# Experts' blocks of 32 places on four column quarters of the array, in a fused attention and mixture-of-experts layer

## The chip, the core and the metric

The kernel runs on one core of a Trainium2 chip. The metric is the device time of one execution in microseconds, lower is better.

## What is computed

One decoder layer on 1024 tokens of width 1024, all float32: RMSNorm, two attention mixers in parallel and their gated merge, then RMSNorm and a routed mixture of 32 experts (SwiGLU, hidden width 512), and a last RMSNorm. The change is in the experts. Each token goes to one group of eight experts and to the best two of them:

```python
gsel = argmax(xt @ w_group + b_group)                  # one of 4 groups
ev, ei = lax.top_k(elog_g, 2)                          # two of its 8 experts
ew = softmax(ev) * gw                                  # their weights
y  = (silu(xb @ w1[e]) * (xb @ w3[e])) @ w2[e]         # for each (token, expert)
out = segment_sum(y * ew)                              # both rows of a token added
```

That makes 2048 pairs of token and expert; how many fall to an expert is known only at run time. W1 and W3 of an expert are 1024 x 512, W2 is 512 x 1024, 2 MB each.

## The kernel before, in words

All engines run hand-written programs that meet at semaphores. What comes before the experts (norms, projections, attention, merge, lines 400 to 900 of the five programs) isn't touched. The routing runs on VectorE tile by tile. GpSimd scatters each token's id into a table in memory, 1024 places for every expert (`scatter_ids`, line 1483), and VectorE adds up how many blocks each expert needs (lines 1322 to 1331, `starts_i`).

A block is up to 64 places (`SLOTS`, line 46) of one expert; every expert has at least one. For each block:

- GpSimd (loop at line 1516) copies the block's ids (1520), gathers its rows of the normed tokens into `xin` (1523), and loads the ids of the next block (`load_ids`, 1510). The rows lie in `hn_d` as two halves of 2 KB, so a block is 128 half rows on 128 partitions. `xin` has one buffer; the gather waits until TensorE has turned the rows before (`x_tr`). Places without a token are left out of the gather.
- TensorE (`expert`, line 844) multiplies the turned rows `xT` with W1 and W3 (line 856): the 64 places are the stationary operand and take half of the array's columns, so that two halves of the weights' columns run side by side, in two PSUM banks. Then it turns the next block's rows (`turn_rows`, 831), turns the hidden rows of its own block (864), and multiplies them with W2 (870).
- ScalarE computes the tanh (`gate_and_rows`, 1026), moves the turned rows out of PSUM (1032), copies the block's output (`put_rows`, 1037) and stores it in `rows_d` with two DMAs (1040). Before the next copy of an output it waits for the landing of that store (`y_st`).
- VectorE forms the SwiGLU product (1364, 1370) and moves the turned hidden rows (1374).

SyncE streams the weights: three experts are held at a time, and `load_expert` (331) for expert e + 3 waits until the blocks of e have used each of W1, W3 and W2. At the end GpSimd gathers two output rows for every token (1532), which are weighted, added and normed.

A float32 matmul stands in the trace as two records.

Of the kernel before, what the change touches and what calls it, by code (L numbers as in the profile page):

```python
# [32 lines left out]
P = 128  # L33
# [12 lines left out]
SLOTS = 64  # L46
MAXB = NE + 2 * SEQ // SLOTS
# [42 lines left out]
def build(nc, t, out):  # L90
# [16 lines left out]
    hn_d = scratch("hn_d", (2 * SEQ, D // 2))  # L107
# [11 lines left out]
    def ba(a, b, pat=None, /, **kw):  # L119
# [73 lines left out]
        we0 we1 we2 we3 we4 we5 we6 we7 we8 x_blk x_tr xT_evac mm1 mm3 tanh_done hid_done hT_ps hT_done y_ps y_evac y_st  # L193
        g_in0 g_in1 fin_in0 fin_in1 fin_in2 fin_in3 fin_in4 fin_in5 fin_in6 fin_in7 g_in2 g_in3 g_in4 g_in5 g_in6 g_in7 comb_std comb_done out_st0 out_st1 act_step h2_st0 h2_st1 gate_in gw_in0 gw_in1 gst0 gst1 hu_done loop_left gelu_arg tanh_gates nsink_done comb_sum gfin_in assigned wdiag_done fin_ps eps_ready wr_ready sel_done first_ps first_ids marks_done second_ps second_ids route_arg route_exp route_ps masks_ready tables y_free""".split()
# [53 lines left out]
    ZPARTS = 8  # L248
    steps_at, tile_done_at = [], {}
# [152 lines left out]
    def _(sp):  # L402
# [54 lines left out]
        for n in range(NGT):  # L457
# [85 lines left out]
    def _(pe):  # L543
# [252 lines left out]
        def first_rows(m):  # L796

            pe.wait_ge(S["sel_done"], m + 1)
            for h in range(2):
                mm = pe.matmul(PS[DH * h:DH * h + DH, 0, 0:2], sel[:, m, :], tok[:, h, m, :],  # L800
                               start=(m == 0), stop=(m == TT - 1), skip_group_check=True)
            return mm
# [18 lines left out]
        pe.wait_ge(S["marks_done"], 1)  # L821
        for m in range(TT):
            for c in range(2):
                for h in range(2):
                    mm = pe.matmul(PS[DH * h:DH * h + DH, 2, 0:2], mark[:, m, c, :], tok[:, h, m, :],
                                   start=(m == 0 and c == 0), stop=(m == TT - 1 and c == 1), skip_group_check=True)
        mm.then_inc(S["second_ps"], 1)
# [16 lines left out]
        def expert(e, nth, par):  # L844
# [715 lines left out]
```

## Time and profile before

| | us |
|---|---|
| median of 3 runs | 1650.41 (1647.76 to 1650.95) |
| the profiled execution | 1650.04 |
| its span, first to last instruction | 1648.4 |
| TensorE busy (matmul) | 1564.9, 95% of the span |
| TensorE weight loads | 848.1, 51% |
| VectorE busy | 560.9, 34% |
| ScalarE busy | 346.8, 21% |
| GpSimd busy | 300.6, 18% |
| DMA in the span | 328.42 MB, mean 199 GB/s |
| mean granted clock of TensorE | 0.988 |

All times are measured from the first instruction. The expert loop fills the stretch from 1050 to 1603 us. The span is 1.6 us shorter than the execution's own time; what the text works out from the trace is set against 1650.04. A busy TensorE is not one at its peak: matmuls overlap, and the records' ends are modelled. "Landing" is the time from the start of a DMA's issue until its semaphore is complete.

### The profile page before, as it was taken

How to read it: one execution, taken by the hardware profiler on the slowest of the kernel's cores; microseconds unless marked ns; L12 is line 12 of the kernel's file. 1: busy time of each engine (PE TensorE's matmuls, PEld its weight loads, DVE VectorE, ACT ScalarE, POOL GpSimd, SP SyncE). 2: the span in 40 equal slices, each digit the busy share in tenths (PEclk: the TensorE clock that was granted, in tenths of full speed). 3: DMA queues.
4: the chain of work that ended last, by engine and by line, in shares of the span. 5: the costliest groups of instructions: out<-in, count | busy, mean ns of one | idle time of the engine just before them, and what ended most of it. 6: DMA issues, size and time to landing. Idle time of an engine off the chain costs nothing.

```text
span 1648.4 us, 21863 instructions
## 1 busy us (share of the span) xinstructions
PE 1564.9 (95%) x7698; PEld 848.1 (51%) x7699; DVE 560.9 (34%) x1542; ACT 346.8 (21%) x859; POOL 300.6 (18%) x431
## 2 busy tenths in 40 slices
PE   7999998999999999998999999799899999999986
PEld 4554544444444444444444555566466666666652
DVE  4210004766566656654222354511011111111115
ACT  3000002443343443433000111111111111111113
POOL 2000001322222222222001001221121212121114
PEclk9999999999999999998999999999999999999997
DMA  9214621553111110103443821699999989999928
GB/s 236 67 56 62 125 78 58 166 181 114 45 32 26 45 33 26 46 13 90 161 136 103 357 107 74 235 416 419 419 419 418 386 352 407 416 421 417 415 85 306
DMA packets 135914, 328.42 MB, mean 199 GB/s; under 512 B 40046, under 2 KB 80398, under 8 KB 126640
## 3 DMA queue, kind: packets, MB, share of 16 engines
q1 hardware_dynamic: 117472, 297.98, 49.5%
q0 software_dynamic: 9984, 17.62, 3.2%
q10 hardware_dynamic: 8400, 12.07, 2.1%
q8 instruction: 34, 0.56, 0.1%
q14 instruction: 24, 0.20, 0.0%
HBM read 276.09 MB, written 55.25 MB: 201 GB/s over the span
## 4 chain that ended last, share of the span: by engine, by line
PE 83%; DVE 7%; DMA 5%; issue 2%; ACT 2%; POOL 1%; SPq 1%; POOLq 0%; ACTq 0%; DVEq 0%
PE PS L856 17%; PE PS L707 12%; PE PS L591 11%; PE PS L870 9%; PE PS L745 7%; PE PS L780 7%; PE PS L693 4%; PE PS L654 4%; PE PS L673 4%; PE PS L586 3%; DMA WA<-w 2%; PE PS L833 2%; DMA BA<-hn_d,ids 1%; POOL WA L1532 1%; PE PS L573 1%
## 5 line engine op out<-in xcount | busy, mean ns | idle before, releaser
L707 PE MATMUL PS<-WA 128*128 128x512 f32 x512 | 255.0, 611 | 2.2 <-ACT WA L967 1.6
L856 PE MATMUL PS<-WA,BA 128*64 128x256 f32 x2048 | 227.6, 379 | 2.9 <-DMA WA<-w 1.5
L856 PEld LDWEIGHTS PS<-WA,BA 128*64 128x64 f32 x2048 | 173.9, 137 | 63.9 <-issue 17.3
L591 PE MATMUL PS<-WA,BA 128*128 128x512 f32 x416 | 180.1, 593 | 2.9 <-DVE WA L1090 2.9
L1450 POOL TENSOR_SCALAR BA<-BA,rin,gates 128x640 f32<-128x640 f32 (+7 forms) x128 | 99.6, 781 | 270.8 <-DVE rin L1209 270.8
L1364 DVE SCALAR_TENSOR_TENSOR BA<-BA,PS 128x256 f32<-128x256 f32 x46 | 19.4, 422 | 340.8 <-ACT BA L1029 340.8
L591 PEld LDWEIGHTS PS<-WA,BA 128*128 128x128 f32 x416 | 78.6, 190 | 99.6 <-issue 96.2
L673 PEld LDWEIGHTS PS<-ident,BA 128*128 128x128 f32 x648 | 79.4, 144 | 94.1 <-issue 86.6
L870 PE MATMUL PS<-WA,BA 128*64 128x512 f32 x512 | 116.9, 597 | 9.7 <-DVE BA L1374 8.7
L707 PEld LDWEIGHTS PS<-WA 128*128 128x128 f32 x512 | 84.6, 190 | 78.4 <-issue 67.6
L957 ACT ACTIVATE BA<-PS,ngm 128x640 f32<-128x640 f32 (+7 forms) x128 | 89.9, 702 | 130.5 <-DVE ngm L1187 126.1
L780 PE MATMUL PS<-BA 128*128 128x512 f32 x256 | 113.1, 595 | 2.3 <-DVE BA L1245 2.3
L673 PE MATMUL PS<-ident,BA 128*128 128x128 f32 x648 | 101.2, 281 | 10.8 <-ACT BA L935 5.5
L745 PE MATMUL PS<-WA 128*128 128x512 f32 x256 | 110.1, 593 | 0.7 <-ACT WA L980 0.7
L856 PE MATMUL PS<-BA 128*64 128x256 f32 x896 | 101.4, 384 | 2.9 <-DMA BA<-w 2.9
L1219 DVE COPY BA<-PS 128x512 f32<-128x512 f32 (+3 forms) x126 | 62.7, 507 | 104.8 <-PE PS L673 104.7
L856 PEld LDWEIGHTS PS<-BA 128*64 128x64 f32 x896 | 76.9, 139 | 30.8 <-issue 8.2
L1186 DVE TENSOR_REDUCE mx<-PS 128x1 f32<-128x640 f32 (+7 forms) x128 | 90.6, 708 | 4.4
L1444 POOL TENSOR_TENSOR BA<-BA,rin 128x512 f32<-128x512 f32 (+1 forms) x32 | 31.5, 986 | 327.8 <-DVE rin L1196 327.8
L654 PE MATMUL PS<-WA 64*128 64x512 f32 (+3 forms) x384 | 75.9, 500 | 7.7 <-DVE pc L1177 4.0
L745 PEld LDWEIGHTS PS<-WA 128*128 128x128 f32 x256 | 48.6, 190 | 62.2 <-issue 60.7
L1520 POOL COPY ids<-ids 128x1 int32<-128x1 int32 x45 | 8.0, 178 | 386.7 <-PE PS L833 272.9
(249 smaller groups left out, 1548.4 us busy)
## 6 DMA issues: line engine op xcount, KB each, us to landing
WA<-w SPq DMA_DIRECT2D x66, 2048.0 KB, 25.3
BA<-w SPq DMA_DIRECT2D x30, 2048.0 KB, 27.6
rows_d<-WA SPq DMA_DIRECT2D x8, 2048.0 KB, 9.5
rows_d<-BA ACTq DMA_DIRECT2D x92, 128.0 KB, 6.8
WA<-w_in SPq DMA_DIRECT2D x16, 512.0 KB, 5.6
gates_d<-WA SPq DMA_DIRECT2D x32, 256.0 KB, 2.4
WA<-gates_d SPq DMA_DIRECT2D x8, 1024.0 KB, 5.4
BA<-w_in SPq DMA_DIRECT2D x26, 256.0 KB, 6.1
```

Source lines behind the costliest of these rows:

```text
L591: mm = pe.matmul(PS[:, j % 4, :], ws[:, c % 6, k, :], hnT[:, k, 512 * h:512 * h + 512], start=(k == 0), stop=(k == KT - 1))
L654: mm = pe.matmul(PS[:, bank, 0:e - a], qb[rows, h, q], kz[rows, w, k0 + a:k0 + e], start=True, stop=True)
L673: mm = pe.transpose(PS[:, 4 + n % 2, P * m:P * m + P], src, ident[:, :])
L693: mm = pe.matmul(PS[DH * g:DH * g + DH, bank, :], v_sb[:, w, kb, DH * g:DH * g + DH], pT[:, SLOT0[br] + n, g, :, :], start=(br == "A" and ...
L707: mm = pe.matmul(PS[:, 6, :], gw[:, j, k, :], hnT[:, k, 512 * hf:512 * hf + 512], start=(k == 0), stop=(k == KT - 1))
L745: mm = pe.matmul(PS[:, b0 + j, :], wbr[:, dt % 2, 4 * j + r, :], o[:, r, sl], start=(r == 0), stop=(r == REP - 1))
L780: mm = pe.matmul(PS[:, 2 * (i % 2) + n, :], mT[:, i, k, :], wout[:, k, 512 * n:512 * n + 512], start=(k == 0), stop=(k == KT - 1))
L856: mm = pe.matmul(PS[DH * h:DH * h + DH, bank, 0:256], xT[:, k, :], w[par][:, k, 256 * h:256 * h + 256], start=(k == 0), stop=(k == KT - 1))
L870: mm = pe.matmul(PS[DH * n:DH * n + DH, 3, :], hT[:, j, SLOTS * h:SLOTS * h + SLOTS], W2[par][:, 2 * h + j, 512 * n:512 * n + 512], start= ...
L957: last = nc.scalar.activation(PB[:, n % 3, 0:nk], src, ACT.Exp, bias=ngm[:, v, 0:1], scale=SC, accum_out=den[:, v, 0:1])
L1186: step(dve.tensor_reduce(mx[:, v, 0:1], s[:, 0:nk], X, ALU.max))
L1450: last = g.tensor_scalar(pr, pr, rin[:, v, 0:1], gates[:, i, col:col + 1], ALU.mult, ALU.mult)
```

## The change

- `SLOTS` is 32, and each expert has at least two blocks (`MAXB` follows).
- The 32 places take a quarter of the array's columns. `hidden_sums` multiplies with both halves of W1 and both of W3 in the four quarters, in one PSUM bank; `put_out` does W2 in four quarters of 256 columns.
- W2 of a block comes after the next block's W1 and W3 and its row transpositions. So the outputs of an expert's last block are computed inside the next expert's program, and once more after the loop.
- `hn_d` holds whole rows of 4 KB. A block's gather is 32 rows on 32 partitions; `turn_rows` is eight transpositions of 32 x 128. The output of a block is copied from PSUM by four copies of 32 x 256 into 32 rows, stored by one DMA.
- ScalarE computes the tanh on 64 partitions; VectorE's products are on 64 partitions, one of each, and one copy moves the turned hidden rows.
- GpSimd waits for the landing of the ids and of the gather before it copies the ids; the next ids' load stands ahead of the gather.
- The routing's second marks (`mark`, `place1`, line 825's matmuls) are gone: one product of selection and token numbers gives the ids of the first 64 places, of which the first two blocks' ids are taken.

The core of the diff; of the programs' loops the added lines are shown, those that go stand in the listing above:

```diff
-SLOTS = 64
-MAXB = NE + 2 * SEQ // SLOTS
+SLOTS = 32
+MAXB = 2 * NE + 2 * SEQ // SLOTS - 2
...
+    xin = BA[0:SLOTS, 8192:9216]
+    xT = ba(9216, 9472, "p (k n) -> p k n", k=KT)
+    xT_ps = PS[:, 7, 0:KT * SLOTS].rearrange("p (k n) -> p k n", k=KT)
+    th = BA[0:FIRST, 9728:9984]
+    hu = BA[FIRST:2 * FIRST, 9984:10240]
+    hv = BA[0:FIRST, 10240:10496]
+    hT = ba(10496, 10624, "p (j n) -> p j n", j=2)
+    hT_ps = PS[:, 2, 0:2 * FIRST].rearrange("p (j n) -> p j n", j=2)
+    ysb = BA[0:SLOTS, 10752:11776]
     fin_h = ba(12288, 20480, "p (t n) -> p t n", t=TT)
     fin_y = wa(0, 16384, "p (t k n) -> p t k n", t=TT, k=2)
...
-                sp.wait_ge(S[("mm1", "mm3", "y_ps")[j]], used)
+                sp.wait_ge(S[("mm13", "mm13", "y_ps")[j]], used)
...
         def turn_rows():
-            for c in range(4):
-                mm = pe.transpose(PS[:, 7, P * c:P * c + P], xin[:, P * c:P * c + P], ident[:, :])
+            for k in range(KT):
+                mm = pe.transpose(xT_ps[:, k, :], xin[:, P * k:P * k + P], ident[0:SLOTS, 0:SLOTS])
...
+        def hidden_sums(b, par, landed):
+            pe.wait_ge(S["xT_evac"], pe.snap(b + 1))
+            for n in range(2):
+                pe.wait_ge(S[f"we{3 * par + n}"], landed)
+            for k in range(KT):
+                for q in range(4):
+                    w = (W1, W3)[q // 2][par]
+                    mm = pe.matmul(PS[SLOTS * q:SLOTS * q + SLOTS, 0, 0:256], xT[:, k, :],
+                                   w[:, k, 256 * (q % 2):256 * (q % 2) + 256], start=(k == 0), stop=(k == KT - 1))
+            mm.then_inc(S["mm13"], 1)
+            pe.wait_ge(S["x_blk"], pe.snap(b * 16 + 32))
+            pe.sem_inc(S["turn_due"], 1)
+            turn_rows()
+        def put_out(n_done, par, landed):
+            pe.wait_ge(S["hT_done"], n_done)
+            pe.wait_ge(S["y_evac"], n_done)
+            pe.wait_ge(S[f"we{3 * par + 2}"], landed)
+            for j in range(2):
+                for h in range(2):
+                    for n in range(4):
+                        mm = pe.matmul(PS[SLOTS * n:SLOTS * n + SLOTS, 3, 0:256], hT[:, j, SLOTS * h:SLOTS * h + SLOTS],
+                                       W2[par][:, 2 * h + j, 256 * n:256 * n + 256],
+                                       start=(j == 0 and h == 0), stop=(j == 1 and h == 1))
+            mm.then_inc(S["y_ps"], 1)
+        def turn_hidden(b):
+            pe.wait_ge(S["hid_done"], pe.snap(b + 1))
+            pe.sem_inc(S["turn_due"], 1)
+            for j in range(2):
+                mm = pe.transpose(hT_ps[:, j, :], hv[:, P * j:P * j + P], ident[0:FIRST, 0:FIRST])
+            mm.then_inc(S["hT_ps"], 1)
+        def expert(e, par, landed, landed_before):
+            lo = pe.value_load(starts_i[0:1, bass.ds(e, 1)], min_val=0, max_val=MAXB - 2)
+            hi = pe.value_load(starts_i[0:1, bass.ds(e + 1, 1)], min_val=2, max_val=MAXB)
+            hidden_sums(lo, par, landed)
+            if landed_before is not None:
+                put_out(lo, (par - 1) % NW, landed_before)
+            turn_hidden(lo)
+            with pe.Fori(lo + 1, hi) as b:
+                hidden_sums(b, par, landed)
+                put_out(b, par, landed)
+                turn_hidden(b)
...
         def gate_and_rows(b):
+            act.wait_ge(S["mm13"], b + 1)
+            nc.scalar.activation(th, PS[0:FIRST, 0, 0:256], ACT.Tanh, scale=0.5).then_inc(S["tanh_done"], 1)
             act.wait_ge(S["x_tr"], b + 3)
...
+            nc.scalar.copy(xT, xT_ps).then_inc(S["xT_evac"], 1)
+        def put_rows(n_done, first):
+            act.wait_ge(S["y_ps"], n_done)
+            for n in range(4):
+                y = nc.scalar.copy(ysb[:, 256 * n:256 * n + 256], PS[SLOTS * n:SLOTS * n + SLOTS, 3, 0:256])
+            y.then_inc(S["y_evac"], 1)
+            act.wait_ge(S["y_evac"], n_done + 1)
+            act.dma_start(rows_d[bass.ds(first, SLOTS), :], ysb).then_inc(S["y_st"], 16)
         gate_and_rows(0)
+        gate_and_rows(1)
+        put_rows(1, 0)
+        with act.Fori(1, act.snap(total - 1)) as b:
+            gate_and_rows(act.snap(b + 1))
+            act.wait_ge(S["y_st"], act.snap(b * 16 + 16))
+            put_rows(act.snap(b + 1), act.snap(b * SLOTS))
+        act.wait_ge(S["y_st"], act.snap(total * 16))
+        put_rows(total, act.snap(total * SLOTS - SLOTS))
+        act.wait_ge(S["y_st"], act.snap(total * 16 + 16))
         act.sem_inc(S["loop_left"], 1)
...
+        total = dve.value_load(starts_i[0:1, NE:NE + 1], min_val=2 * NE, max_val=MAXB)
         with dve.Fori(0, total) as b:
+            dve.wait_ge(S["mm13"], b + 1)
             dve.wait_ge(S["tanh_done"], b + 1)
+            dve.scalar_tensor_tensor(hu, th, 1.0, PS[0:FIRST, 0, 0:256], ALU.add, ALU.mult).then_inc(S["hu_done"], 1)
             dve.wait_ge(S["hu_done"], b + 1)
+            dve.scalar_tensor_tensor(hv, hu, 0.5, PS[FIRST:2 * FIRST, 0, 0:256], ALU.mult, ALU.mult) \
+                .then_inc(S["hid_done"], 1)
+            dve.wait_ge(S["hT_ps"], b + 1)
+            dve.tensor_copy(hT, hT_ps).then_inc(S["hT_done"], 1)
...
-                               allow_slow_non_contiguous=True).then_inc(S["ids_in"], 16)
+            pool.dma_start(ids[0:SLOTS, 0:1], ids_d[bass.ds(row, SLOTS), 0:1],
+                           allow_slow_non_contiguous=True).then_inc(S["ids_in"], 16)
         pool.wait_ge(S["row_tab"], 1)
         load_ids(pool.value_load(block_row_i[0:1, 2:3], min_val=0, max_val=NE * SEQ))
-        total = pool.value_load(starts_i[0:1, NE:NE + 1], min_val=NE, max_val=MAXB)
+        total = pool.value_load(starts_i[0:1, NE:NE + 1], min_val=2 * NE, max_val=MAXB)
+        pool.wait_ge(S["ids_in"], 16)
+        g.tensor_copy(ids[0:SLOTS, 1:2], ids[0:SLOTS, 0:1]).then_inc(S["ids_held"], 1)
         with pool.Fori(2, total + 1) as b:
-            pool.wait_ge(S["ids_in"], pool.snap(b * 32 - 32))
+            pool.wait_ge(S["ids_held"], pool.snap(b - 1))
+            load_ids(pool.value_load(block_row_i[0:1, bass.ds(b + 1, 1)], min_val=0, max_val=NE * SEQ))
             pool.wait_ge(S["x_tr"], pool.snap(b + 1))
             pool.sem_inc(S["rows_due"], 1)
-            g.tensor_copy(ids[:, 1:2], ids[:, 0:1]).then_inc(S["ids_held"], 1)
-            pool.wait_ge(S["ids_held"], pool.snap(b - 1))
+            g.indirect_dma_start(xin, None, hn_d[:, :], bass.IndirectOffsetOnAxis(ap=ids[0:SLOTS, 1:2], axis=0),
+                                 bounds_check=SEQ - 1, oob_is_err=False).then_inc(S["x_blk"], 16)
+            pool.wait_ge(S["ids_in"], pool.snap(b * 16))
+            pool.wait_ge(S["x_blk"], pool.snap(b * 16 + 16))
             pool.sem_inc(S["rows_due"], 1)
-            g.indirect_dma_start(xin[:, :], None, hn_d[:, :], bass.IndirectOffsetOnAxis(ap=ids[:, 1:2], axis=0),
-                                 bounds_check=2 * SEQ - 1, oob_is_err=False).then_inc(S["x_blk"], 16)
-            load_ids(pool.value_load(block_row_i[0:1, bass.ds(b + 1, 1)], min_val=0, max_val=NE * SEQ))
+            g.tensor_copy(ids[0:SLOTS, 1:2], ids[0:SLOTS, 0:1]).then_inc(S["ids_held"], 1)
         pool.wait_ge(S["slots_done"], 1)
```

GpSimd's loop over the blocks before (`BA<-hn_d` is the gather, `ids<-ids_d` the loads of ids, TENSOR_LOAD reads the table of rows; ISA rows are waits and register work):

```order
L1518 REGISTER_ALU
L1520 COPY ids<-ids 128x1
L1521 REGISTER_ALU
L1523 DMA BA<-hn_d,ids 128x512
L1525 ISA
L1525 TENSOR_LOAD BA
L1525 ISA x2
L1510 ISA
L1510 DMA ids<-ids_d 64x1
L1510 ISA
L1510 DMA ids<-ids_d 64x1
```

and GpSimd's loop with the change:

```order
L1523 ISA
L1523 TENSOR_LOAD BA
L1523 ISA x2
L1513 ISA
L1513 DMA ids<-ids_d 32x1
L1524 REGISTER_ALU
L1526 DMA BA<-hn_d,ids 32x1024
L1528 REGISTER_ALU
L1529 REGISTER_ALU
L1531 COPY ids<-ids 32x1
```

The copy of the ids went from ahead of the gather to behind it, and the table's read and the load of ids from behind the gather to ahead of it.

TensorE's program of one block before (`128x128 x4` at L833 turns rows, L864 the hidden rows, L870 is W2):

```order
L856 MATMUL PS<-WA,BA 64x256 x32
L860 ISA
L833 MATMUL PS<-ident,BA 128x128 x4
L863 ISA
L864 MATMUL PS<-ident,BA 128x128
L863 REGISTER_ALU
L864 MATMUL PS<-ident,BA 128x128
L870 MATMUL PS<-WA,BA 64x512 x8
```

and TensorE's with the change, in a block that is not an expert's first (L840 is W1 and W3, L821 turns rows, L855 is W2, L865 turns the hidden rows):

```order
L840 MATMUL PS<-WA,BA 32x256 x32
L843 ISA
L821 MATMUL PS<-ident,BA 128x32 x8
L855 MATMUL PS<-WA,BA 32x256 x16
L865 MATMUL PS<-ident,BA 128x64 x2
```

W2 now stands ahead of the hidden rows' transpositions, and is that of the block before; the matmuls per block are 32 and 16 instead of 32 and 8.

## Rows read from the trace of the kernel before

**Rows 1.** The page, part 2: 40 slices of the span (41.2 us each)

```profile
DMA  9214621553111110103443821699999989999928
GB/s 236 67 56 62 125 78 58 166 181 114 45 32 26 45 33 26 46 13 90 161 136 103 357 107 74 235 416 419 419 419 418 386 352 407 416 421 417 415 85 306
```

**Rows 2.** The chain of waits, 1189 to 1213 us: start, length, what (matmul records)

```profile
1189.70 6.91 PE PS L856 x64
1196.61 0.59 PE PS L833 x4
...
1197.87 3.65 PE PS L870 x16
1201.53 6.91 PE PS L856 x64
```

**Rows 3.** Timeline, first W1 and last W2 block: start, length, what, idle before and releaser

```profile
1050.42 1.95 PE L856 MATMUL PS<-WA,BA 128*64 128x256 f32 x16 [1.32 <-ACT BA L1017]
...
1599.50 3.65 PE L870 MATMUL PS<-WA,BA 128*64 128x512 f32 x16 [0.28 <-DVE BA L1374]
1603.25 0.58 ACT L1037 COPY BA<-PS 128x512 f32<-128x512 f32 x1 [3.79 <-PE PS L870]
```

**Rows 4.** Timeline of TensorE, ahead of the loop

```profile
1031.95 1.10 PE L755 MATMUL PS<-ident,BA 128*128 128x128 f32 x8 [1.15 <-DVE BA L1307]
...
1036.31 0.39 PE L800 MATMUL PS<-winmask,cmpmask 128*64 128x2 bf16 x14
...
1044.69 1.02 PE L825 MATMUL PS<-winmask,BA 128*64 128x2 bf16 x32 [2.42 <-DVE BA L1319]
```

**Rows 5.** Timeline, the turn of one block on ScalarE, VectorE, TensorE and GpSimd

```profile
1205.02 0.38 ACT L1029 ACTIVATE BA<-PS 128x256 f32<-128x256 f32 x1 [2.81 <-PE PS L856]
...
1205.43 0.42 DVE L1364 SCALAR_TENSOR_TENSOR BA<-BA,PS 128x256 f32<-128x256 f32 x1 [7.51 <-ACT BA L1029]
...
1208.88 0.53 PE L864 MATMUL PS<-ident,BA 128*128 128x128 f32 x2
...
1209.45 0.18 POOL L1520 COPY ids<-ids 128x1 int32<-128x1 int32 x1 [8.88 <-DMA ids<-ids_d]
1210.49 1.07 POOL L1523 DMA_INDIRECT BA<-hn_d,ids  x1 [0.86 <-POOL ids L1520]
1211.57 1.08 POOL L1510 DMA_DIRECT2D ids<-ids_d  x2
```

**Rows 6.** Line 1525 (the table entry read), 1100 to 1280 us: count, ns min/median/max

```profile
L1525 POOLq TENSOR_LOAD <-BA x14: 283/287/307, 1109.4 to 1269.5; - x14
```

**Rows 7.** Timeline, a gather right behind another, at the end

```profile
1609.04 0.98 POOL L1532 DMA_INDIRECT WA<-rows_d,slots_i  x1 [0.30 <-issue]
```

**Rows 8.** Line 1523, the row gather, 1100 to 1280 us

```profile
L1523 POOL DMA_INDIRECT BA<-hn_d,ids x14: 1071/1075/1084, 1109.5 to 1269.6; - x14
...
DMA to landing us min/median/max: 5.9/8.3/9.0
```

**Rows 9.** Line 1523 after the last weights, 1572 to 1600 us (2 gathers)

```profile
DMA to landing us min/median/max: 2.2/2.7/3.3
```

**Rows 10.** Line 1040, the store of a block, 1100 to 1280 us

```profile
DMA to landing us min/median/max: 5.6/7.3/10.1
```

**Rows 11.** DMA queues and issues, 1100 to 1280 us

```profile
DMA packets 13397, 75.41 MB, mean 419 GB/s; under 512 B 2472, under 2 KB 2472, under 8 KB 10581
...
q1 hardware_dynamic: 8839, 68.65, 91.6%
...
WA<-w SPq DMA_DIRECT2D x23, 2048.0 KB, 31.3
```

**Rows 12.** Stretches around a wait of TensorE: busy PE, PEld, DVE, ACT, POOL, clock, DMA

```profile
1162.80:1165.20 2.40, 0.28 (x5) 0.21 (x6) 0.42 (x1) 0.38 (x1) 0.00 (x0) 1.00 0.97 383
1165.20:1168.60 3.40, 3.40 (x20) 1.89 (x18) 0.00 (x0) 0.00 (x0) 0.00 (x0) 0.50 1.05 430
```

**Rows 13.** Timeline, the wait in that place

```profile
1164.92 3.42 PE L856 MATMUL PS<-BA 128*64 128x256 f32 x16 [2.12 <-DMA BA<-w]
```

More of the change, by code:

```diff
@@ L798, in first_rows @@
             pe.wait_ge(S["sel_done"], m + 1)
[L799 to L802, printed above, removed]
+            return pe.matmul(PS[0:FIRST, 0, 0:2], sel[:, m, :], tok[:, m, :],
+                             start=(m == 0), stop=(m == TT - 1), skip_group_check=True)
         def keep_busy(count):
@@ L820, in _ @@
         pe.wait_ge(S["h2_done"], TT)
[L821 to L827, printed above, removed]
         keep_busy(10)
         def turn_rows():
-            for c in range(4):
-                mm = pe.transpose(PS[:, 7, P * c:P * c + P], xin[:, P * c:P * c + P], ident[:, :])
+            for k in range(KT):
+                mm = pe.transpose(xT_ps[:, k, :], xin[:, P * k:P * k + P], ident[0:SLOTS, 0:SLOTS])
             mm.then_inc(S["x_tr"], 1)
@@ L875, in _ @@
-        with pe.Fori(0, NE // NW) as e3:
+        def hidden_sums(b, par, landed):
[11 more added lines that the diff above has]
+            turn_rows()
@@ L876, in _ @@
+        for e in range(NW):
+            expert(e, e, 16, None if e == 0 else 16)
+        with pe.Fori(1, NE // NW) as e3:
             for par in range(NW):
-                expert(e3 * NW + par, e3 + 1, par)
+                expert(e3 * NW + par, par, pe.snap(e3 * 16 + 16), pe.snap(e3 * 16 if par == 0 else e3 * 16 + 16))
         for e in range(NE - NE % NW, NE):
-            expert(e, e // NW + 1, e % NW)
+            expert(e, e % NW, 16 * (e // NW + 1), 16 * ((e - 1) // NW + 1))
+        total = pe.value_load(starts_i[0:1, NE:NE + 1], min_val=2 * NE, max_val=MAXB)
@@ L1016, in _ @@
         act.wait_ge(S["x_tr"], 2)
-        nc.scalar.copy(xT_out, xT_ps).then_inc(S["xT_evac"], 1)
+        nc.scalar.copy(xT, xT_ps).then_inc(S["xT_evac"], 1)
         act.wait_ge(S["route_arg"], 1)
@@ L1285, in place @@
                 dve.wait_ge(S["first_ps"], 1)
-                dve.tensor_scalar(ids[:, 2:3], PS[:, 0, 0:1], PS[:, 0, 1:2], None, ALU.add).then_inc(S["first_ids"], 1)
+                for n in range(2):
+                    rows = slice(SLOTS * n, SLOTS * n + SLOTS)
+                    dve.tensor_scalar(ids[0:SLOTS, 2 + n:3 + n], PS[rows, 0, 0:1], PS[rows, 0, 1:2], None, ALU.add) \
+                        .then_inc(S["first_ids"], 1)
             step(dve.tensor_reduce(slot_f[:, m, :], pick, X, ALU.add))
@@ L1332, in _ @@
         dve.sem_inc(S["routed"], 1)
-        dve.wait_ge(S["second_ps"], 1)
-        dve.tensor_scalar(ids[:, 3:4], PS[:, 2, 0:1], PS[:, 2, 1:2], None, ALU.add).then_inc(S["second_ids"], 1)
         step(dve.tensor_tensor(G4[3][:, :, :], lgs[:, :, 0:NG], top[:, 0, :].unsqueeze(2).to_broadcast([P, TT, NG]), ALU.subtract))
@@ L1495, in _ @@
         scatter_ids(TT - 2)
-        pool.wait_ge(S["first_ids"], 1)
+        pool.wait_ge(S["first_ids"], 2)
         pool.wait_ge(S["hn_st"], 16 * TT)
-        g.indirect_dma_start(xin[:, :], None, hn_d[:, :], bass.IndirectOffsetOnAxis(ap=ids[:, 2:3], axis=0)) \
+        g.indirect_dma_start(xin, None, hn_d[:, :], bass.IndirectOffsetOnAxis(ap=ids[0:SLOTS, 2:3], axis=0)) \
             .then_inc(S["x_blk"], 16)
         scatter_ids(TT - 1)
-        pool.wait_ge(S["second_ids"], 1)
         pool.wait_ge(S["x_tr"], 2)
-        g.indirect_dma_start(xin[:, :], None, hn_d[:, :], bass.IndirectOffsetOnAxis(ap=ids[:, 3:4], axis=0)) \
+        g.indirect_dma_start(xin, None, hn_d[:, :], bass.IndirectOffsetOnAxis(ap=ids[0:SLOTS, 3:4], axis=0)) \
             .then_inc(S["x_blk"], 16)
```

116 lines of the change are left out of this document (22 added, 94 removed).

## The prediction

> **What bounds the kernel now.** I read the page's slices first, for where the time is, then the chain of waits over the expert loop, then what hides behind the chain: GpSimd's turn of one block and the landings of its DMAs.
>
> The slices [rows 1] show two things at once in the last third: the DMA engines are at 9 tenths and move about 419 GB/s, and this lasts for all of the expert loop. The chain [rows 2] shows one block of 64 places as 6.91 us of W1 and W3 (64 matmul records, two abreast, so 0.216 us per pair of records), 0.59 us of row transpositions, some 0.66 us for the hidden rows, and 3.65 us of W2 (16 records): 11.83 us from 1189.70 to 1201.53. The loop has 46 such blocks, from 1050.42 to 1599.50 + 3.65 = 1603.15 [rows 3], which is 552.7 us. 46 x 11.81 = 543.3; the other 9.4 are waits for weights. So TensorE sets the time, with the weights' DMA close behind it.
>
> What must be seen for this change is work that is hidden now. GpSimd copies the ids, then issues the gather 0.86 us later, then the loads of the next ids [rows 5]. The gather lands 8.3 us (median of 14; 5.9 to 9.0) after its start while weights stream [rows 8], and 2.2 to 3.3 us after it when they don't [rows 9]. One gather of 64 places is allowed 11.8 us today, so this shows nowhere as a wait of TensorE.
>
> **Number of blocks.** 46 blocks at 64 places with at least one for each of 32 experts means 14 experts with more than 64 places. Routing the reference's inputs gives 38 to 61 places to the other 18 and 66 to 94 to those 14. With 32 places and at least two blocks that is 18 x 2 + 14 x 3 = **78 blocks**. (The same 2048 places are filled; 2496 are computed, before 2944.)
>
> **TensorE's time for a block.** W1 and W3 still make 64 records of 256 columns, now four abreast: 16 x 0.216 = 3.46 us. No row shows four abreast. The bounds are 6.91 (two abreast, as now [rows 2]) and 3.46; I take the latter, since a pass of 256 columns takes its 0.216 us with the columns of both halves in use, and 32 short matmuls in 1.02 us [rows 4] show that four records can be issued in 0.13 us. The Trainium skill (TensorEngine Tiling (Array Packing), Tiling Modes) gives 128x32 as four tiles that run independently; no run here shows that. W2 is 32 records of 256 columns: 8 x 0.216 = 1.73 us. The eight row transpositions of 32 places lie between 8 x 0.028 = 0.2 us (the short matmuls of line 800) and 1.10 us (eight of 128x128 at line 755) [rows 4]; they load 128 columns each like the latter, I take 0.9. The two of the hidden rows: 0.4, from 0.53 for two wider ones [rows 5]. Sum 3.46 + 1.73 + 0.9 + 0.4 = **6.5 us**, and 78 x 6.5 = 507 us.
>
> The hidden rows' own chain (tanh 0.38, two products of 0.42 [rows 5], three handovers of about 0.1) is 1.5 us. It starts with the end of W1 and W3 and lies behind the row transpositions and W2 of the block before, 0.9 + 1.7 = 2.6 us: the wait of 0.3 us before W2 in each block [rows 3] goes, and it costs nothing as long as that cover stands.
>
> **The gather's round trip.** This is where the change adds a wait. xin has one buffer. In the new loop of GpSimd the copy of the ids waits for the landing of the gather before it, the load of the next ids stands between that copy and the next gather, and with them a read of the table. From a landing to the next gather's start: 0.25 us to the copy (semaphore and two queue instructions), 0.18 the copy, 0.86 until the next instruction that needs it [rows 5], 0.6 the table read (0.29 [rows 6] and the register work behind it), 0.55 the load of ids (half of 1.08 [rows 5]), 0.4 for the gather's own start (0.30 between two gathers [rows 7], and one more wait). That is 2.9 us; from below 1.9, if the table read and the start lie beside other work. Before, only 0.18 + 0.86 stood there.
>
> Then the landing. The gather has 32 rows of 4 KB instead of 128 of 2 KB. Bounds under weights: 8.3 us (nothing gained [rows 8]) and 5.6 us (the fastest store of 64 rows of 2 KB, the same 128 KB [rows 10]; its median is 7.3). I take 6.5, in the lower half, because the number of rows is a quarter. So a block takes 2.9 + 6.5 = **9.4 us** where weights stream, with bounds 1.9 + 5.6 = 7.5 and 2.9 + 8.3 = 11.2, and TensorE waits at line 821 (the row transpositions), holding W2 of the block before, the hidden rows and the next block. Where no weights stream the round trip is 2.9 + 2.3 = 5.2 us (2.3, near the shorter of the two landings [rows 9], for the fewer rows), less than 6.5: no wait.
>
> The weights of an expert are 6.29 MB. Their queue moved 68.65 MB in 180 us [rows 11], 381 GB/s, so they stream for 16.5 us per expert. TensorE needs 78 / 32 = 2.44 blocks, 15.9 us, without any wait; with waits it is slower than the weights, so these catch up, three experts are held, and each of the last 29 loads starts when an expert's buffers come free and ends before the next do. In 16.5 us there are 16.5 / 9.4 = 1.75 blocks, each 2.9 us over 6.5: 5.1 us. The rows of the first of them have landed up to 6.5 - 5.2 = 1.3 us early: 3.8 us remain. 29 x 3.8 = 110 us.
>
> **The clock.** After a wait of 2.12 us [rows 13] in a stretch at full clock, TensorE ran at 0.50 of it (1.2 GHz of 2.4) for 3.4 us [rows 12], which is 1.7 us of work lost. Waits of that length come once or twice per expert in this forecast. I count one, and half of it hidden in the next wait: 29 x 0.85 = 25 us. Bounds: 0, and 50 waits of 1.7 us, 85.
>
> **The rest.** The store: landing, four copies of 32 x 256 (0.38 each, from the 0.38 of line 1029 [rows 5], 1.5 together), 0.2 to the DMA, landing between 5.6 and 7.3: about 8.1 us, under 9.4 and hidden. It is what comes next if the gather turns out shorter than I say. The removed marks and 32 short matmuls (1.02 us, after 2.42 of waiting [rows 4]) let the loop start about 2 us earlier; the last block's four copies end 0.6 later than one of 0.58 [rows 3]. Bytes of the gathers are the same, stores shrink from 12.1 to 10.2 MB: not on the path. The value reads of each expert on TensorE's queue are issued while W2 runs: nothing.
>
> **The sum.** Loop 507 + 110 + 25 = 642 us against 552.7: +89. With -2 and +0.6 it is +88. The profiled execution took 1650.0 (span 1648.4), the median of the runs is 1650.4, so the two are alike: **1738 us**. A measurement of this kernel can't tell less than about 0.2% (3.3 us) from no change.
>
> **The rivals.**
>
> *A: the gather is short enough and the quarters pay (faster).* If the landing falls under 6.5 - 2.9 = 3.6 us with weights streaming, TensorE is never kept waiting: loop 507 + 9.4 = 516, time 1650 - 37 - 1 = 1612. From that landing on it decides. For it: landings of 2.2 to 3.3 us when the queues are empty [rows 9]. Against it: none of the 14 under load is below 5.9 [rows 8], and stores half their size aren't below 5.6 [rows 10]. The Trainium skill (DMA: Bandwidth & Descriptors, Anatomy of one DMA — SWDGE (gpsimd) path) fits a GpSimd DMA as 2.0 us and its bytes at 436 GB/s, which is an estimate of 2.3 us for 128 KB and would give this rival; rows 9 agree with it, rows 8 don't. The same page (Queues, rings and completion order) has each DMA engine go round the queues packet by packet, which fits the landings under load. Chance 0.08, of which 0.01 for a time within 0.2%.
>
> *B: the clock goes with the waits.* Every block that waits is followed by 3.4 us at half clock and nothing of it is hidden: 85 instead of 25, 1798 us. For it: the one such place seen [rows 12, 13]. Against: while the clock is low, the wait itself is shorter. Chance 0.10.
>
> *C: the quarters don't run four abreast.* Then the change doesn't do what it says: 6.91 + 3.45 + 1.3 = 11.7 us for each of 78 blocks, 913 us, time about 2010. Chance 0.03.
>
> The forecast keeps 0.79.
>
> **How the numbers follow.** The low end is a gather cycle of 8.2 us and no loss by the clock: 16.5 / 8.2 = 2.0 blocks x 1.7 = 3.4, less 1.3, x 29 = 61; loop 568; 1665. The high end takes in rival B, 1800. The two ends leave out A, C and the tails of the forecast, 2 in 10. Faster by over 0.2%: 0.08; within 0.2%: 0.01; slower by over 0.2%: 0.91.
>
> **What would show it.** Right: 78 blocks; groups of W1 and W3 in about 3.5 us; TensorE idle before the row transpositions with the gather as releaser, some 3 us, in one or two blocks of each expert and not in all; a gather landing of 5.5 to 7 us under load; the weights' queue with pauses, SyncE waiting for buffers, mean DMA rate in the loop near 330 GB/s; half-clock stretches in the loop. Wrong: a landing under 4 us, or GpSimd's path from a landing to the next gather under 2 us (then towards A); TensorE waiting in every block, weights streaming or not; the store as last releaser; W1 and W3 in 6.9 us.

## The result and the profile after

The changed kernel takes **1763.9 us** (median of 4 runs, 1762.6 to 1787.0) against 1650.7 us of the kernel before, a ratio of 1.072 (1.064 to 1.079). The forecast was 1738 us, its range 1665 to 1800. The profiled execution took 1787.0 (span 1785.3), the slowest of the four, so the sums below are made against its own loop. Of all executions in this document one, of the kernel with two tiles for the rows behind gathers two ahead, took 1816.9 us at a granted clock of 0.84 and is left out of its ratio.

The page of the changed kernel, part 2, its slices (44.6 us each), and part 4, the start of the chain's lines; the slices answer to [rows 1]:

```profile
PEclk9999999999999999999999988889899898998898
DMA  9124704441111110026383249898878788977747
GB/s 250 29 71 56 170 0 158 162 152 40 27 30 42 30 42 25 18 77 213 105 322 131 96 179 347 322 354 351 309 283 304 302 323 340 392 281 288 269 136 285
...
DMA BA<-hn_d,ids 21%; PE PS L704 11%; PE PS L588 10%; PE PS L777 6%; PE PS L742 5%; PE PS L840 5%; PE PS L690 4%; PE PS L651 4%; PE PS L855 4%; PE PS L670 3%; PE PS L583 2%; PE PS L821 2%; POOLq L1523 1%; POOL WA L1538 1%; PE PS L570 1%
```

The loop's DMA rate has fallen from 419 to some 310 GB/s, TensorE's clock has eights in it, and the row gather has a fifth of the chain. Two blocks show it all (timeline of the changed kernel; it answers to [rows 2, 5, 13]):

```profile
1304.25 0.65 PE L821 MATMUL PS<-ident,BA 32*128 32x32 f32 x8 [1.55 <-DMA BA<-hn_d,ids]
1304.28 0.18 POOL L1531 COPY ids<-ids 32x1 int32<-32x1 int32 x1 [6.91 <-DMA BA<-hn_d,ids]
1304.84 1.93 PE L855 MATMUL PS<-BA 128*32 128x256 f32 x32
...
1305.87 0.54 POOL L1513 DMA_DIRECT2D ids<-ids_d  x1 [1.41 <-issue]
1306.70 0.34 PE L865 MATMUL PS<-ident,BA 64*128 64x64 f32 x2
1306.77 0.95 POOL L1526 DMA_INDIRECT BA<-hn_d,ids  x1 [0.36 <-issue]
...
1306.97 3.66 PE L840 MATMUL PS<-WA,BA 128*32 128x256 f32 x64
...
1313.38 0.65 PE L821 MATMUL PS<-ident,BA 32*128 32x32 f32 x8 [2.75 <-DMA BA<-hn_d,ids]
1313.40 0.18 POOL L1531 COPY ids<-ids 32x1 int32<-32x1 int32 x1 [5.68 <-DMA BA<-hn_d,ids]
1313.96 2.94 PE L855 MATMUL PS<-WA,BA 128*32 128x256 f32 x32
```

W1 and W3 take 3.66 us: four abreast. The gather of 1306.77 lets GpSimd go on at 1313.40, 6.6 us later, and TensorE has stood still for 2.75 us. W2, 1.93 us before, then takes 2.94, in a stretch whose granted clock is 0.63 (the columns are those of [rows 12]; the second row is W1 and W3 ahead of the wait, at full clock). From one copy of ids to the next gather it is 1306.77 - 1304.28 = 2.5 us. The two stretches:

```profile
1314.00:1316.80 2.80, 2.80 (x33) 1.16 (x32) 0.00 (x0) 0.37 (x1) 1.45 (x2) 0.63 0.18 70
1306.97:1310.60 3.63, 3.63 (x66) 1.97 (x64) 0.29 (x1) 1.32 (x4) 0.75 (x1) 1.00 0.92 327
```

All landings of 1100 to 1700 us (line 1526; answers to [rows 8]) and TensorE's waits in the loop (engine, line, releaser: total, times, longest):

```profile
DMA to landing us min/median/max: 2.8/6.8/8.6
```

```profile
PE PS L821 <- DMA BA<-hn_d,ids: 108.7, 48, 3.9
PE PS L840 <- issue: 18.5, 20, 1.4
```

The loop as one stretch, of before and of the changed kernel, from the first W1 to the last W2 before and to the start of the last block after (stretch, length, busy PE, PEld, DVE, ACT, POOL, clock, DMA share, GB/s):

```profile
1050.40:1603.20 552.80, 533.33 (x3956) 340.67 (x3956) 67.45 (x244) 71.60 (x140) 107.08 (x183) 1.00 0.94 381
```

```profile
1051.30:1730.30 679.00, 551.53 (x8130) 313.00 (x8131) 90.52 (x245) 168.54 (x458) 128.52 (x233) 0.90 0.81 309
```

551.5 us busy and 128 us of waits are the 679. What the 551.5 would be at full clock, the run without the weights' loads tells.

### The profile page after: what moved, and what is told of

The parts are those of the page before. It is cut to its first block, busy times and chain, and to the rows that moved or that the text cites. A ratio compares the mean times of both kernels' runs of the same rounds, so it can differ in the third digit from the quotient of the medians.

```text
span 1785.3 us, 31566 instructions
## 1 busy us (share of the span) xinstructions
PE 1590.7 (89%) x11974; PEld 823.4 (46%) x11975; DVE 583.9 (33%) x1543; ACT 447.6 (25%) x1189; POOL 320.2 (18%) x482
## 4 chain that ended last, share of the span: by engine, by line
PE 60%; DMA 22%; issue 7%; DVE 6%; POOLq 2%; ACT 1%; POOL 1%; SPq 0%; ACTq 0%; DVEq 0%
DMA BA<-hn_d,ids 21%; PE PS L704 11%; PE PS L588 10%; PE PS L777 6%; PE PS L742 5%; PE PS L840 5%; PE PS L690 4%; PE PS L651 4%; PE PS L855 4%; PE PS L670 3%; PE PS L583 2%; PE PS L821 2%; POOLq L1523 1%; POOL WA L1538 1%; PE PS L570 1%
## 5 line engine op out<-in xcount | busy, mean ns | idle before, releaser
L840 PE MATMUL PS<-WA,BA 128*32 128x256 f32 x3456 | 205.2, 390 | 14.7 <-issue 14.1
L1049 ACT COPY BA<-PS 32x256 f32<-32x256 f32 x312 | 113.7, 364 | 179.1 <-PE PS L855 134.9
L821 PE MATMUL PS<-ident,BA 32*128 32x32 f32 x632 | 57.4, 234 | 111.3 <-DMA BA<-hn_d,ids 111.3
L840 PEld LDWEIGHTS PS<-WA,BA 128*32 128x32 f32 x3456 | 115.7, 113 | 83.8 <-issue 23.4
L1375 DVE SCALAR_TENSOR_TENSOR BA<-BA,PS 64x256 f32<-64x256 f32 x78 | 32.4, 415 | 325.0 <-ACT BA L1041 325.0
L855 PE MATMUL PS<-WA,BA 128*32 128x256 f32 x1728 | 136.5, 470 | 1.4 <-issue 1.4
L704 PEld LDWEIGHTS PS<-WA 128*128 128x128 f32 x512 | 84.6, 190 | 78.5 <-issue 67.6
L821 PEld LDWEIGHTS PS<-ident,BA 32*128 32x128 f32 x632 | 49.7, 150 | 145.8 <-issue 145.8
L1380 DVE COPY BA<-PS 128x128 f32<-128x128 f32 x78 | 22.8, 292 | 265.9 <-PE PS L865 265.9
L840 PE MATMUL PS<-BA 128*32 128x256 f32 x1536 | 91.8, 393 | 4.5 <-issue 4.5
```

Of the source, the lines that this page charges most:

```text
L704: mm = pe.matmul(PS[:, 6, :], gw[:, j, k, :], hnT[:, k, 512 * hf:512 * hf + 512], start=(k == 0), stop=(k == KT - 1))
L821: mm = pe.transpose(xT_ps[:, k, :], xin[:, P * k:P * k + P], ident[0:SLOTS, 0:SLOTS])
L840: mm = pe.matmul(PS[SLOTS * q:SLOTS * q + SLOTS, 0, 0:256], xT[:, k, :], w[:, k, 256 * (q % 2):256 * (q % 2) + 256], start=(k == 0), stop= ...
L855: mm = pe.matmul(PS[SLOTS * n:SLOTS * n + SLOTS, 3, 0:256], hT[:, j, SLOTS * h:SLOTS * h + SLOTS], W2[par][:, 2 * h + j, 256 * n:256 * n + ...
L1049: y = nc.scalar.copy(ysb[:, 256 * n:256 * n + 256], PS[SLOTS * n:SLOTS * n + SLOTS, 3, 0:256])
```

## Experiments

My theory T after the result: the gather's round trip (landing, copy, table read, load of ids, gather) paces the blocks in which weights stream, and the low clock follows from its waits. Rivals: TensorE's own quarters are slower than counted, with the weights' stream beside them or at all (R1), the store's round trip is the real pace (R2), the clock falls for another reason, or one of the change's other pieces costs the time.

**The changed kernel again,** beside the experiments.

> The changed kernel once more, unchanged, since its own profiled execution took 1786.95 us and its others 1762.6 to 1764.2. Theory T (the gather's round trip under the weights' traffic, in an xin of one buffer, keeps TensorE waiting, and the waits pull the clock down): about 1763 us; some 46 to 50 waits of TensorE before the row transpositions, about 110 us together, and between 115 and 145 us of the loop at half clock. If the extra 23 us of the first profile are more half-clock time, a profile at 1763 has some 45 us less of it or shorter waits. Rival R1 (TensorE's own quarters are slower than counted): waits are few and the block cycle without wait is over 8 us. Rival R2 (the store of a block holds ScalarE and through it TensorE): waits of ScalarE's copies for rows_d's landing are the long ones.

Measured: 1771.7 us (ratio 1.074, 1.071 to 1.077), with 42 gather waits of 97.0 us together and 552.4 us busy in its loop of 673.5 us. Its granted clock there was 0.89; if all of the lack is half clock, that is 673.5 x 0.11 x 2, an estimate of 148 us, just over my range. Below, "the changed kernel" is 1763.9 to 1771.7 us, and its gather waits are 97.0 to 108.7.

**Without the weights' loads.** SyncE's loads of the experts after the third are left out, and TensorE's waits for them; the other experts compute with stale weights.

```diff
-        with sp.Fori(1, NE // NW) as e3:
-            for par in range(NW):
-                reload(e3 * NW + par, par)
-        for e in range(NE - NE % NW, NE):
-            reload(e, e % NW)
...
```

> Leaves out the loads of the weights of experts 3 to 31: every expert is computed with the first three experts' weights, so that no weights stream during the loop; all else is the same. T: gathers land in 2 to 3 us, the round trip is 5.2 us, TensorE has no wait before the row transpositions, the clock stays at 2.4 GHz, a block takes 6.5 to 6.7 us, the loop 510 to 520 us, the whole 1605 to 1620 us. R1: the block cycle stays at 8 us or more, 1730 us or more. R2: the store's round trip also shortens, so this run alone does not tell R2 from T.

Measured: 1630.2 us (ratio 0.988, 0.986 to 0.990). Its loop stretch, and a piece of TensorE's timeline:

```profile
1053.60:1575.70 522.10, 490.32 (x8132) 298.51 (x8132) 90.58 (x245) 168.56 (x458) 128.58 (x233) 1.00 0.19 52
```

```profile
1305.93 3.66 PE L835 MATMUL PS<-WA,BA 128*32 128x256 f32 x64
1309.52 0.68 PE L816 MATMUL PS<-ident,BA 32*128 32x32 f32 x8
1310.12 1.93 PE L850 MATMUL PS<-WA,BA 128*32 128x256 f32 x32
1311.99 0.33 PE L860 MATMUL PS<-ident,BA 64*128 64x64 f32 x2
1312.25 3.66 PE L835 MATMUL PS<-WA,BA 128*32 128x256 f32 x64
...
1319.38 3.66 PE L835 MATMUL PS<-WA,BA 128*32 128x256 f32 x64 [0.73 <-issue]
```

Without the stream the round trip is short and TensorE waits for a gather only twice; the clock is full. A block is 1312.25 - 1305.93 = 6.32 us, where R1 wanted 8 or more. W1 and W3 take 3.66 us here as they do in the changed kernel while the DMA engines are 0.92 busy (1306.97 above, clock 1.00), so a busy stream did not slow them there, and the 490.3 us busy here, for the same records as 551.5, price the clock in the changed kernel: **61 us**. What my range missed is the wait at an expert's first W1, 26 us in 30 places, where nothing but TensorE's own queue (two table reads and a loop's end) stands before it: the 10 us over my range.

**Without the ids.** GpSimd's load and copy of ids are left out; every block gathers the same 32 rows.

```diff
-            load_ids(pool.value_load(block_row_i[0:1, bass.ds(b + 1, 1)], min_val=0, max_val=NE * SEQ))
...
-            g.indirect_dma_start(xin, None, hn_d[:, :], bass.IndirectOffsetOnAxis(ap=ids[0:SLOTS, 1:2], axis=0),
+            g.indirect_dma_start(xin, None, hn_d[:, :], bass.IndirectOffsetOnAxis(ap=ids[0:SLOTS, 3:4], axis=0),
...
-            pool.wait_ge(S["ids_in"], pool.snap(b * 16))
-            pool.wait_ge(S["x_blk"], pool.snap(b * 16 + 16))
...
-            g.tensor_copy(ids[0:SLOTS, 1:2], ids[0:SLOTS, 0:1]).then_inc(S["ids_held"], 1)
```

> Leaves out, on GpSimd, the load and the copy of each block's ids: all gathers from block 2 on use block 1's ids (32 real rows each), so the next gather starts as soon as TensorE has turned the rows before. The landings stay as they are. T: of the 2.66 us from a landing to the next gather about 1.6 remain (turned rows 0.75, semaphore and start 0.8), about 1.1 us less for each of some 46 waiting blocks and less half-clock time: 40 to 75 us less, 1690 to 1725 us. R1 and R2: no change, 1755 to 1770 us.

Measured: 1751.2 us (ratio 1.061, 1.059 to 1.063), 13 to 20 less than the changed kernel: over my range, and just under that of the rivals. GpSimd's path from a landing to the next gather went only from 2.66 to 1.64 us: xin must be turned by TensorE before it is filled again (0.65 at 1304.78, and 0.9 from its end to the gather):

```profile
1304.78 0.65 PE L821 MATMUL PS<-ident,BA 32*128 32x32 f32 x8 [0.50 <-DMA BA<-hn_d,ids]
1305.36 1.93 PE L855 MATMUL PS<-WA,BA 128*32 128x256 f32 x32
1306.29 0.91 POOL L1521 DMA_INDIRECT BA<-hn_d,ids  x1 [5.96 <-PE PS L821]
```

TensorE's waits for the gather were 80.6 us, 16 to 28 less than in the changed kernel's two profiles, and its clock's loss 538.3 - 490.3 = 48, 13 to 14 less. (All of its 32 rows are fetched in every block, more bytes than before.) So the load of ids is a minor part of the cycle; the single buffer and the landing are the rest.

**The ids' load behind the gather,** as the kernel before has it, with all of the work done.

```diff
-            load_ids(pool.value_load(block_row_i[0:1, bass.ds(b + 1, 1)], min_val=0, max_val=NE * SEQ))
             pool.wait_ge(S["x_tr"], pool.snap(b + 1))
             pool.sem_inc(S["rows_due"], 1)
             g.indirect_dma_start(...)
+            load_ids(pool.value_load(block_row_i[0:1, bass.ds(b + 1, 1)], min_val=0, max_val=NE * SEQ))
```

> The changed kernel with the load of the next ids put back behind the gather, as the kernel before has it. Theory T (the 2.66 us from a landing to the next gather is part of the cycle that TensorE waits for): the path shrinks to the 1.64 us of the run without ids, where only the row transpositions stand in it, so each of the 1.75 blocks per expert that wait is 1.0 us shorter, 29 x 1.75 x 1.0 = 51 us at the most; the run without ids, which had the same path, gave 13 to 20 us back: 1735 to 1755 us. Rival I (the ids, started 1.9 us after the gather and landing 4 to 6.6 us later, now land last and take the place of what was saved): GpSimd waits for the ids' landing, the path from the gather's landing stays over 2.3 us, 1760 to 1785 us.

Measured: 1764.5 us (ratio 1.069, 1.065 to 1.072), not to be told from the changed kernel. GpSimd's timeline and its waits in the loop show rival I:

```profile
1309.45 0.96 POOL L1525 DMA_INDIRECT BA<-hn_d,ids  x1 [1.85 <-PE PS L821]
1310.54 0.54 POOL L1513 DMA_DIRECT2D ids<-ids_d  x1
1318.22 0.18 POOL L1531 COPY ids<-ids 32x1 int32<-32x1 int32 x1 [7.15 <-DMA ids<-ids_d]
1319.44 0.95 POOL L1525 DMA_INDIRECT BA<-hn_d,ids  x1 [1.04 <-issue]
```

```profile
POOL ids L1531 <- DMA ids<-ids_d: 368.5, 77, 8.7
```

128 bytes of ids, asked for 1.1 us behind the rows, took over 7 us to arrive, and in all 77 blocks they landed last. In the changed kernel the same copy waited for the gather all 76 times. So with the stream running the 128 bytes were as late as the 128 KB of rows, and the load of ids costs something in either place: behind the rows it lands last, and ahead of them it stands in the way from one landing to the next gather.

**Gathers two ahead.** Two landing buffers on free columns, four columns of ids; GpSimd copies a landed block into xin (1.03 us) and issues the gather of the block after the next.

```diff
+                pool.wait_ge(S[f"land{j % 2}"], pool.snap(i * 32 + 16 * (j // 2) + 16))
+                pool.wait_ge(S["x_tr"], pool.snap(i * 4 + j + 3))
+                g.tensor_copy(xin, xland[j % 2]).then_inc(S["rows_rdy"], 1)
...
+                gather(c)
```

> The same computation with the round trip hidden: GpSimd gathers two blocks ahead into two landing buffers with a semaphore each, ids are loaded four blocks ahead, and a landed block is copied by GpSimd into xin (32 x 1024, some 1 to 1.5 us) when its rows are due. T: no wait before the row transpositions except the copy's, the weights' DMA and TensorE (6.5 us a block) bound the loop together: 510 to 540 us, 1610 to 1640 us, below the kernel before (1650). R1: 1730 us or more. R2: the store takes over: some 8 us a block under traffic, 1700 us or more.

Measured: 1702.0 us (ratio 1.032, 1.029 to 1.034). That is 62 to 70 us less than the changed kernel, with the gather gone from TensorE's waits: so much of the loss was the gather's. But T's range, 1610 to 1640, was missed by 62, and the time lies in the range of R2. What comes next is worth nearly as much. The waits in its loop:

```profile
DVE BA L1379 <- ACT BA L1045: 426.8, 78, 7.8
POOL BA L1540 <- PE PS L823: 303.4, 76, 7.9
ACT BA L1053 <- DMA rows_d<-BA: 289.9, 68, 6.3
```

ScalarE waits 68 times for the store of the block before; behind that wait in its queue stands the next block's tanh, and behind the tanh VectorE and TensorE. That last link is read from the programs: TensorE's own rows name VectorE for 7.6 us only and no releaser for 65. The next run tests it.

**Gathers two ahead, and two tiles for the finished rows.**

```diff
-    ysb = BA[0:SLOTS, 10752:11776]
+    ysb = [BA[SLOTS * i:SLOTS * i + SLOTS, 10752:11776] for i in range(2)]
...
+                act.wait_ge(S[("hn_st", "y_st")[p]], act.snap(i * 16 + (128, 32)[p]))
+                put_rows(act.snap(i * 2 + p + 2), act.snap(i * 2 * SLOTS + p * SLOTS + SLOTS), 1 - p)
```

> The gathers two blocks ahead, and now two tiles for the finished rows as well, so that ScalarE's copy waits for the store of the block before the last. Theory S (with the gather out of the way the store's round trip set the pace: ScalarE waited 292 us for stores, 69 times, and TensorE then for ScalarE's and VectorE's late work): those waits fall under 40 us, the block's cycle from 7.67 us to 7.0 to 7.3 us, being 6.5 of TensorE's work plus issue gaps and what the clock still costs, so 1702 - 77 x 0.4 to 0.7 = 1650 to 1675 us, clock over 0.98. Rival D (the weights, gathers and stores together are what the queues can move, 355 GB/s in that loop, and the store's wait only shows it): the waits turn up at the weights or the gathers instead, 1690 to 1705 us.

Measured: **1650.7 us** (ratio 0.9999, 0.9989 to 1.0009): the kernel before's time to 0.1%. Theory S holds, with the time at the low edge of its range, and D falls. The loop stretch, TensorE's waits in it, and the queues of 1100 to 1500 us (answers to [rows 11]):

```profile
1054.70:1595.30 540.60, 497.37 (x8130) 298.81 (x8130) 90.51 (x245) 168.75 (x458) 196.62 (x236) 0.98 0.99 387
```

```profile
PE PS L842 <- issue: 21.5, 24, 1.4
PE PS L842 <- DMA WA<-w: 9.7, 4, 3.3
PE PS L842 <- DMA BA<-w: 7.5, 3, 4.3
```

```profile
DMA packets 26113, 159.80 MB, mean 400 GB/s; under 512 B 5063, under 2 KB 5063, under 8 KB 20127
...
q1 hardware_dynamic: 18935, 146.43, 91.5%
```

ScalarE has no wait for a store any more. TensorE still has 17 us of waits for weights, and the DMA engines are full (0.99): 541 us for 32 experts is 16.9 us for each, against the 16.5 us that an expert's weights stream. So TensorE's 490 us are under the weights' time now, and by these rates less of TensorE's work would hardly show as time; no run tried it.

**Two tiles for the rows alone,** the last diff put into the changed kernel, whose gathers stay as they are.

> The changed kernel with two tiles for the finished rows and nothing else. Theory T (the gather's round trip sets the changed kernel's pace, the store is only next behind it): ScalarE's waits for stores, 39 us over 17 blocks, go, but lie mostly in blocks that wait for the gather anyway: 1745 to 1765 us. Rival S (store and gather take turns in setting the pace): at least the 39 us come back, under 1728 us.

Measured: 1778.1 us (ratio 1.079, 1.071 to 1.086), 13 us over T's range and not faster; its runs (1768.9 to 1794.4) overlap those of the changed kernel. S is out: ScalarE's waits for stores are gone, and TensorE's for the gather are 103.7 us. The same edit is worth 51 us on top of the two-ahead gathers and nothing without them.

**Each store as two DMAs of 2 KB runs.**

```diff
-            act.dma_start(rows_d[bass.ds(first, SLOTS), :], ysb).then_inc(S["y_st"], 16)
+            for n in range(2):
+                cols = slice(512 * n, 512 * n + 512)
+                act.dma_start(rows_d[bass.ds(first, SLOTS), cols], ysb[:, cols]).then_inc(S["y_st"], 16)
...
```

> The changed kernel with each block's store in two DMAs, of 32 rows of 2 KB each, in place of one of 32 rows of 4 KB. Theory T (the store is hidden behind the gather's cycle, and runs of 4 KB are worth nothing by themselves): 1760 to 1780 us, ScalarE's waits for stores at 40 to 80 us instead of 39. Rival P (twice the packets crowd the gathers too): gather landings under load rise from 7.3 us, 1790 us or more.

Measured: 1768.8 us (ratio 1.071, 1.069 to 1.073). Its wait is larger than I said, and costs nothing:

```profile
ACT BA L1049 <- DMA rows_d<-BA: 168.9, 49, 6.1
```

It took no time because TensorE waited for the gather meanwhile (96.7 us). The gathers weren't crowded, as P wanted: they landed in 6.5 us (median; 2.3 to 8.4). That the length of the runs matters where the store is the pace isn't excluded; it wasn't tried there.

**Filling the wait.** 14 transpositions of the unit matrix behind W1 and W3.

```diff
             mm.then_inc(S["mm13"], 1)
+            keep_busy(14)
             pe.wait_ge(S["x_blk"], pe.snap(b * 16 + 32))
```

> The changed kernel with 14 transpositions of the unit matrix, 0.145 us each or 2.0 us, between a block's W1 and W3 and its wait for the gather. In the 29 or so blocks that wait 3.9 us they lie in the wait, in the 48 others they add up to 2.0 us each, 96 us. Theory K (TensorE's low clock, 140 us of the loop at half speed and so 70 us lost, comes from these waits): the half-clock time falls under 40 us and 50 us or more come back, so 1764 + 96 - 50 to 70 = 1790 to 1810 us, clock over 0.98. Rival (the low clock comes from something else): half-clock time stays over 100 us and the time is 1840 to 1865 us.

Measured: 1831.2 us (ratio 1.110, 1.107 to 1.112), 21 us over the range of theory K, and yet K's mechanism holds:

```profile
1306.71 1.75 PE L802 MATMUL PS<-ident 128*128 128x128 f32 x14
```

```profile
1050.60:1772.40 721.80, 639.46 (x9208) 415.00 (x9208) 90.54 (x245) 168.00 (x457) 128.50 (x233) 0.97 0.77 290
```

The fill is 78 x 1.75 = 137 us. 639.5 - 137 - 490.3 = 12 us is left as the clock's loss, against 61: the low clock came from the idle time. The time went up because the fill took only 26 to 37 us out of the gather's waits (71.2 left), and cost the other 100 or more.

**W2 behind its own block's W1 and W3,** that piece of the change undone.

```diff
-            hidden_sums(lo, par, landed)
-            if landed_before is not None:
-                put_out(lo, (par - 1) % NW, landed_before)
-            turn_hidden(lo)
-            with pe.Fori(lo + 1, hi) as b:
+            with pe.Fori(lo, hi) as b:
                 hidden_sums(b, par, landed)
-                put_out(b, par, landed)
                 turn_hidden(b)
+                put_out(pe.snap(b + 1), par, landed)
...
```

> The changed kernel with W2 put back behind the same block's W1 and W3. A block that doesn't wait for its gather then waits for tanh, the two products, the turn and its copy: 1.5 us to the hidden rows less 0.65 of row transpositions, and 0.5 for the turned copy, 1.3 us. Theory T: 48 blocks pay this, 62 us, the 29 that wait for the gather pay nothing, since the gather runs on meanwhile: 1800 to 1826 us, with the gather waits falling from 111 us to 75 to 95. Rival (the gather's cycle is the pace of nearly all blocks, and this piece of the change is worth nothing): 1755 to 1775 us.

Measured: 1831.2 us (ratio 1.110, 1.108 to 1.112), 5 us over the range of T. TensorE's waits in its loop:

```profile
PE PS L865 <- DVE BA L1371: 55.7, 65, 1.0
PE PS L855 <- DVE BA L1374: 47.7, 66, 1.3
PE PS L821 <- DMA BA<-hn_d,ids: 24.0, 25, 3.4
```

The hidden rows' chain costs 103 us of waits, 73 to 85 us of the gather's are gone in exchange (I had said that 75 to 95 would be left; 24.0 are), and the clock's loss is 579.0 - 490.3 = 89, which is 27 to 28 more. So this piece of the change is worth 60 to 67 us to the changed kernel by the medians (45 to 52 by the profiled executions), a good part of it by the clock.

## Why the prediction was right, and where not

The direction, the mechanism and the place were right: one or two waits of some 3 us for each expert before the row transpositions, released by the gather, because a single xin is filled in a round trip that is longer than a block of 32 places. They were 48 (29 of them of 2 us and over), of 2.3 us in the mean. The sum ran 26 us short of the median, and 49 us short of the profiled execution. Against the latter, term by term (loop up to the last block's start, forecast 77 x 6.5 + 110 + 25 = 635.5, measured 679.0):

| term | forecast | measured |
|---|---|---|
| blocks | 78 | 78 |
| TensorE's block at full clock | 6.5 us (3.46 + 1.73 + 0.9 + 0.4) | 6.32 us (3.66, 1.93, 0.68, 0.33, overlapping a little) |
| TensorE's work to the last start | 500.5 us | 490.3 us |
| waits for the gather | 110 us | 108.7 us, 48 times |
| **clock** | **25 us (0 to 85)** | **61 us** |
| waits of TensorE's own queue | 0 | 19 us |

- **The step that was mis-sized is the clock.** "I count one, and half of it hidden in the next wait: 29 x 0.85" took the loss behind one wait of before [rows 12], 1.7 us, for one wait in each expert. There were 48 waits and 61 us, 1.3 us for each: less was hidden than I took, and more waits set it off. The 61 lie within my bounds and nearer to rival B's 85 than to the 25.
- **"The value reads ... nothing"** was wrong: 18.5 us here, 26 us where nothing else waits, 0.9 us at an expert's first W1.
- **The waits** came out within 2 us, partly by luck (a second profile of the same kernel has 97.0): the landing under load was longer than my 6.5 (46 of 76 took over 5 us, 7.3 in the mean), the path from landing to gather shorter than my 2.9 (2.66 us, 2.5 of it behind the copy's start), together 10.0 instead of 9.4. That the sum came out all the same isn't explained by a run of its own; a block at half clock is longer, and so waits less.
- **Rival A** (short landings) fell: the gathers of the run without weights landed in 2.4 to 6.1 us, median 2.9, and it is the stream that makes them 6.8. Its price, 1612 us, left the weights out: the run without their loads took 1630.2, and the one in which they stream and neither gather nor store is waited for 1650.7. By the fit of the Trainium skill (DMA: Bandwidth & Descriptors, Anatomy of one DMA — SWDGE (gpsimd) path), an estimate of 2.3 us, the landings without the stream are near and those beside it are not. **Rival C** fell with 3.66 us.
- **The store** was named as what comes next at 8.1 us, and it was (68 waits once the gather was out of the way).
- **Two readings of the loop before** were off, and neither enters the sum. Of the 9.4 us that I called waits for weights the trace has 5.4 as such. And the gather did show as a wait of TensorE, twice, 1.4 us together. The 0.2% that I gave as the least difference to be told holds for the kernel before; the changed one's runs lie up to 1.4% apart.
- The DMA rate of the loop was forecast near 330 GB/s, and was 309. The start, forecast 2 us earlier, was 1 us later (1048.6 to 1054.7 us over the runs, whose programs up to there are the same); from the last W2's end to the span's end it was 45.3 us, against 45.2 before, where I had 0.6 more.

## What to carry to other kernels

Smaller blocks save work on the engine that bounds (here 533 us busy for the 46 blocks before, 490 at full clock for 77 of the 78) and shorten the time that hides every round trip. So before blocks are halved, write down for each round trip in the loop (gather, dependent ids, store) its length under the real load and give each the buffers that the shorter block needs; here both the gather and the store had to be given theirs before the change broke even, and each alone showed 62 to 70 us or nothing. Then ask what the saved work uncovers: with the waits for gather and store gone the kernel was only back at 1650.7 us, and the DMA engines were full. The weights' stream had been close behind TensorE all along. And price a new wait of TensorE with its clock: in these runs 109 us of waits brought another 61.

## What I had not expected of the hardware

- 128 bytes of ids landed in 3.9 us (median; 1.7 to 6.5) ahead of the gather and in 5.6 us (1.9 to 9.0) behind it, while the weights' stream ran in turns.
- The clock's loss followed the gather's waits. In six profiles without fill (the changed kernel twice, without the ids, ids behind, half stores, two tiles alone) 80.6 to 108.7 us of these waits went with 48 to 66 us of loss, 0.56 to 0.64 us for each us waited. It didn't follow the number of waits or any wait alike: 89 us for 156 waits of 127 us (W2 in its own block), 12 us for 50 waits of 71 us where fill stood ahead of them, 7 us (497.4 - 490.3) for the 43 us of idle time that were left with both round trips hidden. The granted clocks were 0.90 in the changed kernel's loop and 0.86, 0.97 and 0.98 in the last three, means between the levels of 2.4 and 1.2 GHz.
- 64 records of 128 x 32 times 256 columns take 3.66 us with four quarters abreast, at full clock; eight transpositions that load 128 columns and stream 32 take 0.68 us.
